# A hybrid decoder layer: the overflow tile is computed ahead of the last expert, whose rows are added by TensorE

## The chip, the cores and the metric

The kernel runs on one core of a Trainium2 chip. The metric is the device time of one execution in microseconds (us), lower is better. Times are medians of a few runs; one more execution was recorded by the hardware profiler, and all rows below are of that one.

## The reference, cut to what matters

One decoder layer over 1024 positions of width 1024. After the token mixing (not touched here) comes a mixture of experts: each position picks 1 of 4 groups and in it 2 of 8 experts, 32 in all, with a hidden width of 128. All data are float32.

```
x  = x + gt1 * y                                   # token mixing
h2 = rms_norm(x, norm2_g) * (1 + sc2) + sh2
hg = einsum('nd,edf->nef', h2, w_gate)
hu = einsum('nd,edf->nef', h2, w_up)
act = silu(hg) * hu * gates                        # gates: 2 of 32 are not zero
x  = x + gt2 * einsum('nef,efd->nd', act, w_down)
return rms_norm(x, final_g)
```

## The kernel before

There is no scheduler: each engine has its own program, written out by hand, and the programs meet at semaphores. The order on an engine is the order of the code.

*Before the experts.* The rows x1 (the sum of input and token mixing) are stored in DRAM as `y_d`, their normed form as `xn2_d`. A router gives each expert a list of up to 128 positions (`tbl`, one column for each expert). What does not fit in an expert's 128 goes into overflow tiles: their lists are scattered to `far_d` during the expert loop and reloaded into further columns of `tbl`. Their number is `n_ov`, read from memory at run time. In the measured data the loop over them makes one turn.

*The expert loop*, 32 turns, `TURN[e]` being the expert of turn e. TensorE transposes the gathered 128 rows (`ex_t`), ScalarE and VectorE scale and shift them (`modulated`), TensorE makes the gate and up products (`ex_gu`: thirty-two 128x128 matmuls in the trace), ScalarE and VectorE the activation (`hidden`), TensorE the down product (`ex_dn`: two 128x512 products, four matmuls in the trace), VectorE multiplies by the router's gate and gt2 into `yo[e % 3]` (`result`), and GpSimd adds the rows to `y_d` by an indirect DMA (`scatter_add`). GpSimd also issues the gathers, up to four turns ahead (`gather_behind`). TensorE's order in a turn is transposes of e + 1, gate and up of e, down of e - 1.

*Weights.* SP issues three 512 KB transfers for each turn into a ring of 11 places (`load_expert`); a turn waits until all three have landed. For the overflow tile SP waits for `ov_go`, which GpSimd raises at turn 27, and loads into place 0.

*The overflow loop* follows turn 31 on every engine: gate and up, activation, down, scaling, scatter. The tile of E + 1, transposed in the loop for a next turn, holds no rows if there is none. Before its scatter GpSimd waits for all scatters of the 32 experts.

*The end.* When the overflow scatter has landed, `f_go` is raised, and SP reads `y_d` back in eight tiles of 128 rows into `x1[:, j]`. For each tile ScalarE squares and sums (1024 columns), for each pair of tiles VectorE adds EPS and GpSimd takes the power -0.5, VectorE scales each tile by the root and `final_g`, SP stores it.

`banks` is PSUM (8 banks, `PS[i]`); REG_P, REG_W, REG_Y and REG_S are large SBUF areas that many tiles share, so the trace names them and not the tiles. L792 is TensorE's `mm` helper, L1434 ScalarE's `fn`, L498 the direct weight loads, L500 those of the overflow tile, L531 the reload of `tbl`, L723 the gather, L729 the scatter, L2244 the scaling in `result`, L2281 the last scaling.

## Time and profile before

| | us |
|---|---|
| median of 3 runs (lowest to highest) | 873.35 (871.69 to 873.62) |
| profiled execution, its own time | 874.96 |
| its span, first to last instruction | 873.2 |
| TensorE busy in it | 815.8 |
| VectorE / ScalarE / GpSimd busy in it | 460.3 / 240.4 / 278.8 |

The span is what the trace shows; the execution's own time also has what lies around it. Positions in the trace are us from the span's start. The first 630 us are token mixing and router, the expert loop follows until about 834, then come the overflow tile and the end.

### The profile page before, as it was taken

Reading aid. Unit: us, or ns where it says so; the run is one execution under the profiler, and the core shown is the slowest. Engines: PE = TensorE matmul, PEld = TensorE weight load, DVE = VectorE, ACT = ScalarE, POOL = GpSimd, SP = SyncE. Lnnn points to the kernel's source line nnn. Section 1 sums busy time; section 2 is a strip of 40 time slices with the busy share of each in tenths; the row PEclk is TensorE's granted clock in tenths of the full one; section 3 lists DMA queues with packets and bytes.
Section 4 is the critical chain, followed back from the end, with each engine's and each line's share of the span. In section 5 each row is a group of like instructions: output and inputs, shape, how many; then the busy total and the mean of one; then the engine's idle time right before and its main releaser. Section 6 shows DMA issues by size and latency. Waiting matters only on the chain. (4 is left out here: it accounts for less than half of the span.)

```text
span 873.2 us, 17369 instructions
## 1 busy us (share of the span) xinstructions
PE 815.8 (93%) x7175; PEld 544.7 (62%) x7175; DVE 460.3 (53%) x1154; ACT 240.4 (28%) x581; POOL 278.8 (32%) x267
## 2 busy tenths in 40 slices
PE   8999999999999999799888999999999999999950
PEld 8557544544444355777777455555788888888830
DVE  3750478887830136467664244434645555454534
ACT  6220111112200143455543112221233223232214
POOL 5810000000499501452741100000135565543332
PEclk9999999999999999999999999999999999999995
DMA  9934433445111123000000881112889989888639
GB/s 315 324 90 135 145 120 121 139 158 172 37 38 36 27 70 133 18 3 4 4 4 20 308 325 48 49 73 96 325 296 301 303 285 273 277 267 261 206 73 367
DMA packets 79719, 136.35 MB, mean 156 GB/s; under 512 B 17213, under 2 KB 51226, under 8 KB 79642
## 3 DMA queue, kind: packets, MB, share of 16 engines
q1 hardware_dynamic: 69338, 118.44, 39.0%
q0 software_dynamic: 10304, 16.82, 8.2%
q8 instruction: 57, 0.93, 0.5%
q14 instruction: 20, 0.16, 0.1%
HBM read 124.18 MB, written 29.92 MB: 176 GB/s over the span
## 5 line engine op out<-in xcount | busy, mean ns | idle before, releaser
L792 PE MATMUL banks<-REG_W 128*128 128x512 f32 (+2 forms) x832 | 274.6, 499 | 0.9 <-DVE pend L1988 0.5
L792 PEld LDWEIGHTS banks<-REG_W 128*128 128x128 f32 (+1 forms) x832 | 125.9, 182 | 135.3 <-issue 133.8
L792 PE MATMUL banks<-REG_W,REG_Y 128*128 128x512 f32 x256 | 118.3, 599 | 1.4 <-DVE REG_Y L2236 1.1
L1434 ACT ACTIVATE REG_P<-banks 128x256 f32<-128x256 f32 (+2 forms) x126 | 53.5, 463 | 156.8 <-PE banks L792 137.7
L792 PE MATMUL banks<-REG_P 64*64 64x64 f32 (+3 forms) x2752 | 79.5, 230 | 13.1 <-issue 8.9
L792 PEld LDWEIGHTS banks<-REG_P 64*64 64x64 f32 (+1 forms) x2752 | 67.6, 135 | 23.0 <-issue 16.4
L1434 ACT ACTIVATE REG_Y<-banks,mod,s 128x128 f32<-128x128 f32 x136 | 51.2, 457 | 85.8 <-PE banks L1386 85.8
L792 PEld LDWEIGHTS banks<-REG_W,REG_Y 128*128 128x128 f32 x256 | 45.6, 191 | 44.3 <-issue 44.2
L792 PEld LDWEIGHTS banks<-REG_Y,REG_P 128*128 128x128 f32 (+1 forms) x616 | 63.1, 181 | 7.0 <-issue 7.0
L792 PE MATMUL banks<-REG_Y,REG_P 128*128 128x128 f32 (+1 forms) x616 | 66.6, 276 | 0.1
L636 POOL TENSOR_TENSOR REG_P<-REG_P 128x1040 f32<-128x1040 f32 x2 | 4.8, 2390 | 175.8 <-DVE REG_P L1801 175.8
L792 PE MATMUL banks<-REG_Y,REG_W 128*128 128x128 f32 x512 | 59.9, 275 | 0.2 <-DVE REG_Y L2105 0.2
L792 PEld LDWEIGHTS banks<-REG_Y,REG_W 128*128 128x128 f32 x512 | 58.4, 192 | 1.1 <-DMA REG_W<-in_moe_w_down 1.1
L1715 DVE SCALAR_TENSOR_TENSOR REG_Y<-REG_P,cc,REG_Y 128x256 f32<-128x256 f32 x112 | 54.3, 485 | 4.0
L729 POOL DMA_INDIRECT y_d<-REG_Y,tbl x22 | 34.9, 1589 | 60.0 <-DVE REG_Y L2244 60.0
L678 POOL TENSOR_TENSOR REG_P<-REG_P,lmask 128x512 f32<-128x512 f32 x20 | 26.3, 1322 | 79.7 <-DVE REG_P L2014 79.7
L792 PE MATMUL banks<-REG_P,REG_Y 128*128 128x512 f32 x112 | 51.4, 592 | 0.0
L2105 DVE TENSOR_SCALAR REG_Y<-banks,s,mod 128x128 f32<-128x128 f32 x136 | 46.2, 403 | 2.0 <-PE banks L1386 2.0
L579 POOL TENSOR_SCALAR ss<-ss 128x1 f32<-128x1 f32 x16 | 3.6, 224 | 135.9 <-ACT REG_P L1434 127.8
L2233 DVE SCALAR_TENSOR_TENSOR REG_Y<-REG_Y,banks 128x128 f32<-128x128 f32 x33 | 9.5, 288 | 70.8 <-ACT REG_Y L1434 70.8
L2244 DVE SCALAR_TENSOR_TENSOR REG_Y<-banks,tbl,gtb 128x512 f32<-128x512 f32 x46 | 32.4, 746 | 19.2 <-PE banks L792 19.2
L1434 ACT ACTIVATE REG_Y<-banks 128x128 f32<-128x128 f32 (+2 forms) x43 | 14.8, 345 | 88.4 <-PE banks L792 76.5
(295 smaller groups left out, 1108.1 us busy)
## 6 DMA issues: line engine op xcount, KB each, us to landing
REG_P<-in_w_ada SPq DMA_DIRECT2D x20, 1024.0 KB, 6.2
REG_W<-in_w_in SPq DMA_DIRECT2D x17, 512.0 KB
REG_P<-in_moe_w_gate SPq DMA_DIRECT2D x17, 512.0 KB, 8.3
REG_W<-in_moe_w_gate SPq DMA_DIRECT2D x16, 512.0 KB, 6.4
REG_W<-in_moe_w_up SPq DMA_DIRECT2D x16, 512.0 KB, 10.7
REG_W<-in_moe_w_down SPq DMA_DIRECT2D x16, 512.0 KB, 16.7
REG_P<-in_moe_w_up SPq DMA_DIRECT2D x14, 512.0 KB, 14.9
REG_P<-in_moe_w_down SPq DMA_DIRECT2D x12, 512.0 KB, 21.2
```

The lines of the kernel that those rows point to most:

```text
L579: ch.step(gp.tensor_scalar(sj, sj, EPS, None, ALU.add))
L636: ch.step(gp.tensor_tensor(zc, zc, yc, ALU.mult))
L678: gp.tensor_tensor(bl[:, l % 2], ab[:, :, 0, :], lmask[:, l:l + 1, :].to_broadcast([P, 8, CH]), ALU.mult)\
L729: gp.indirect_dma_start(out=y_d[:, :], out_offset=bass.IndirectOffsetOnAxis(ap=at, axis=0), in_=yo[b], in_offset=None, bounds_check=last_r ...
L792: return pe.matmul(o_, l, r, start=start, stop=stop, skip_group_check=True)
L1434: return act.activation(o_, i_, f, **kw)
L1715: last = stt(dst, src[:, k], cc[:, k:k + 1], dst, ALU.mult, ALU.add)
L2105: last = ts(dst[:, k, :], PS[bank][:, (k - 4) * P:(k - 3) * P], s2[:, k:k + 1], mod[:, M_SH2 + k:M_SH2 + k + 1], ALU.mult, ALU.add)
L2233: ch.step(stt(a1[:, par, :], th[:, par, :], 1.0, PS[2 + par][:, 0:P], ALU.add, ALU.mult))
L2244: last = stt(yo[b][:, h * 512:(h + 1) * 512], PS[4 + 2 * par + h][:, :], gate(TURN[e] if isinstance(e, int) else e), gtb[:, 1, h * 512:(h ...
```

## The change

What it does, engine by engine:

- The overflow loop stands between turn 30 and turn 31 (`LAST`). Its scaled rows go to `yo[2]`. The counts of its semaphores are one lower, those of turn 31 come after it.
- Turn 31 is not scattered. VectorE builds eight 128x128 matrices `hot[:, j]` of ones and zeros (1 where a row of expert 31's tile belongs to position p of tile j). After turn 31, TensorE multiplies `hot[:, j]` with expert 31's scaled rows into a pair of PSUM banks, for each of the eight tiles.
- For tiles 0, 2, 4, 5, 6, 7 VectorE adds that pair to the tile read back from `y_d` (`completed`). For tiles 1 and 3 (`ON_PE`) TensorE adds the tile itself, by a product with the identity (`reloaded`), and ScalarE and VectorE read the sum from PSUM.
- `y_d` is read back once the overflow scatter has landed (`ov_go`; `f_go` is gone).
- The roots are taken tile by tile on GpSimd, in two instructions each (`rstd`), where one served two tiles.
- The gather of the overflow tile is issued at turn 25 (before: 28), the reload of `tbl` ahead of the weights of turn 30 (before: ahead of those of turn 31), and the gather for the tile after it before the scatter of turn 30. `xg[3]` is cleared once.

```diff
@@ sp @@
             for e in range(RING, E):
                 sp.wait_ge(s["m_dn"], e - RING + 1)
-                load_expert(e % RING, TURN[e], s_w[e % RING])
                 if e == E - 2:
                     sp.wait_ge(s["far_tab"], 16 * 2 * NT)
                     sp.dma_start(tbl[:, E:TILES, :], far_d.rearrange("(p t) c -> p t c", t=OVT)).then_inc(s["far_ld"], 16)
+                load_expert(e % RING, TURN[e], s_w[e % RING])
...
-            sp.wait_ge(s["f_go"], 1)
+            sp.wait_ge(s["ov_go"], n_ov + 1)
@@ gpsimd @@
+            ch.step(gp.memset(xg[3], 0.0))
+            gather(TURN[3], 3)
...
-            for e in range(E):
+            for e in range(LAST):
+                if e == LAST - 1:
+                    gp.wait_ge(s["m_tx"], E + 1)
+                    gather(E + 1, 0)
                 gp.wait_ge(s["m_yd"], e + 1)
                 scatter_add(rows_of(TURN[e], 0), e % RES)
                 gather_behind(e + 3)
-                if e == E - 1:
-                    gp.wait_ge(s["m_tx"], E + 1)
-                    gather(E + 1, 0)
-                if e + BUF == E:
+                if e + 3 + BUF == E:
                     gp.wait_ge(s["far_ld"], 32)
                     gp.wait_ge(s["m_tx"], E - BUF + 1)
                     gather(E, 0)
...
+            for j in range(NT):
+                rstd(j, 2)
@@ tensor @@
             ex_t(E, 0, 16 * (E // BUF + 1))
-            ex_dn(E - 1, (E - 1) % 2, (E - 1) % RING)
+            ex_dn(LAST - 1, 0, (LAST - 1) % RING)
...
             with pe.Fori(0, n_ov) as i:
                 ex_gu(i + E, 0, 0, "m_", s["ov_w"], i * 48 + 48, False)
-                pe.wait_ge(s["m_yd"], i + E)
-                ex_dn(i + E, 0, 0, "m_", False)
                 ex_t(i + (E + 1), 0, i * 16 + 16 * (E // BUF + 2))
+                pe.wait_ge(s["m_yd"], i + LAST)
+                ex_dn(i + LAST, 0, 0, "m_", False)
+
+            ex_gu(LAST, 1, LAST % RING, wsem=s_w[LAST % RING], wcount=w_loads(LAST % RING, LAST // RING + 1), wait_free=False)
+            ex_dn(n_ov + LAST, 1, LAST % RING, wait_free=False)
+            beside(8, 2)
+            def placed(j):
+                q = 2 * ((j + 1) % 4)
...
+                if j - 4 in ON_PE:
+                    pe.wait_ge(s["f_o"], j - 3)
+                elif j >= 4:
+                    pe.wait_ge(s["op_x1"], NT + 1 + [i for i in FIN if i not in ON_PE].index(j - 4))
+                for h in range(2):
+                    if j == 0:
+                        pe.wait_ge(s["m_yd"], n_ov + (E + h))
+                    last = mm(PS[q + h][:, :], hot[:, j, :], yo[LAST % RES][:, h * 512:(h + 1) * 512], True, j not in ON_PE)
+                return last
+
+            def reloaded(j):
+                q = 2 * ((j + 1) % 4)
+                pe.wait_ge(s_w[j], w_loads(j, len(range(j, E, RING))) + 16)
+                for h in range(2):
+                    last = mm(PS[q + h][:, :], ident[:, :], x1[:, j, h * 512:(h + 1) * 512], False, True)
+                return last
@@ vector @@
+            ch.step(dve.tensor_copy(gap[:, 0:1], tbl[:, TURN[LAST], 0:1]))
+            ch.step(stt(left[:, :], i32[:, 0:NT], -float(P), gap[:, 0:1].to_broadcast([P, NT]), ALU.mult, ALU.add))
+            for j in range(NT):
+                ts(hot[:, j, :].rearrange("p (a b) -> p a b", a=KD), i128[:, :].rearrange("p (b a) -> p a b", a=KD), left[:, j:j + 1], None, ALU.is_equal)
...
+            def completed(j):
+                dve.wait_ge(s_w[j], w_loads(j, len(range(j, E, RING))) + 16)
+                dve.wait_ge(s["op_ps"], NT + 1 + FIN.index(j))
+                tt(x1[:, j], x1[:, j], pair(j), ALU.add).then_inc(s["op_x1"], 1)
```

How the order of instructions changes is shown at three places. First TensorE's queue of before, from the down products of turn 29 to the end. `ident` is the transpose of a tile, `128x512 x2` a down product; the names are of the SBUF areas.

```order
L792 MATMUL banks<-REG_W,REG_Y 128x512 x2
L792 MATMUL banks<-REG_Y,REG_P 128x128 x16
L792 MATMUL banks<-REG_S,REG_Y 128x512 x2
L1386 MATMUL banks<-ident,REG_Y 128x128 x8
L792 MATMUL banks<-REG_P,REG_Y 128x512 x2
L1423 TENSOR_LOAD idy
...
L792 MATMUL banks<-REG_Y,REG_W 128x128 x16
...
L792 MATMUL banks<-REG_W,REG_Y 128x512 x2
...
L1386 MATMUL banks<-ident,REG_Y 128x128 x8
```

The same stretch of the changed kernel, up to the placement of tile 3:

```order
L795 MATMUL banks<-REG_W,REG_Y 128x512 x2
L1389 MATMUL banks<-ident,REG_Y 128x128 x8
L795 MATMUL banks<-REG_S,REG_Y 128x512 x2
L1425 TENSOR_LOAD idy
...
L795 MATMUL banks<-REG_Y,REG_W 128x128 x16
...
L1389 MATMUL banks<-ident,REG_Y 128x128 x8
...
L795 MATMUL banks<-REG_W,REG_Y 128x512 x2
...
L795 MATMUL banks<-REG_Y,REG_P 128x128 x16
...
L795 MATMUL banks<-REG_P,REG_Y 128x512 x2
...
L795 MATMUL banks<-REG_Y,REG_W 128x512 x5
L795 MATMUL banks<-REG_P,ident 128x512 x2
L795 MATMUL banks<-REG_Y,REG_W 128x512 x2
```

Turn 31's gate and up products (`REG_Y,REG_P`, x16) have moved from ahead of turn 30's down product to behind the overflow tile, and its down product with them; the transposes in the loop stand ahead of the overflow tile's down product, and the 128x512 products at the end are new.

Second, VectorE's queue of the changed kernel from the scaling of turn 31 (L2280) on; in the kernel before, eight L2281 scalings and four L2273 additions stand there.

```order
L2280 SCALAR_TENSOR_TENSOR REG_Y<-banks,tbl,gtb 128x512 x2
L2328 TENSOR_TENSOR REG_P<-REG_P,banks 128x1024 x2
L2332 SCALAR_TENSOR_TENSOR REG_P<-REG_P,rs,gtb 128x1024
L2332 SCALAR_TENSOR_TENSOR REG_P<-banks,rs,gtb 128x1024
L2328 TENSOR_TENSOR REG_P<-REG_P,banks 128x1024
L2332 SCALAR_TENSOR_TENSOR REG_P<-REG_P,rs,gtb 128x1024
L2328 TENSOR_TENSOR REG_P<-REG_P,banks 128x1024
L2332 SCALAR_TENSOR_TENSOR REG_P<-banks,rs,gtb 128x1024
L2328 TENSOR_TENSOR REG_P<-REG_P,banks 128x1024
L2332 SCALAR_TENSOR_TENSOR REG_P<-REG_P,rs,gtb 128x1024
L2328 TENSOR_TENSOR REG_P<-REG_P,banks 128x1024
L2332 SCALAR_TENSOR_TENSOR REG_P<-REG_P,rs,gtb 128x1024 x3
```

The six additions (L2328) alternate with the eight last scalings (L2332); from tile 4's on there are four additions and six scalings. Third, SP's queue in the changed kernel, between the weights of turns 29 and 30; before, the row `tbl<-far_d` stood behind the row with REG_S.

```order
L503 DMA REG_W<-in_moe_w_down 128x1024
L535 DMA tbl<-far_d 128x30
L503 DMA REG_P<-in_moe_w_gate 128x1024
L503 DMA REG_Y<-in_moe_w_up 128x1024
L503 DMA REG_S<-in_moe_w_down 128x1024
```

The reload of `tbl` has moved ahead of the three transfers of turn 30.

## Rows read from the trace of the kernel before

**Rows 1.** Page of the profile: span, busy time of each engine, granted clock in 40 slices.
```profile
span 873.2 us, 17369 instructions
...
PE 815.8 (93%) x7175; PEld 544.7 (62%) x7175; DVE 460.3 (53%) x1154; ACT 240.4 (28%) x581; POOL 278.8 (32%) x267
...
PEclk9999999999999999999999999999999999999995
```

**Rows 2.** Timeline, 800 to 846 us: start us, duration us, engine, line, operation, count.
```profile
805.78 1.88 PE L792 MATMUL banks<-REG_P,REG_Y 128*128 128x512 f32 x4
807.50 1.04 PE L1386 MATMUL banks<-ident,REG_Y 128*128 128x128 f32 x8
...
823.59 1.06 POOL L723 DMA_INDIRECT REG_Y<-xn_d,tbl  x1 [0.30 <-issue]
...
824.28 1.88 PE L792 MATMUL banks<-REG_W,REG_Y 128*128 128x512 f32 x4
...
831.76 1.09 PE L1386 MATMUL banks<-ident,REG_Y 128*128 128x128 f32 x8
832.69 1.88 PE L792 MATMUL banks<-REG_P,REG_Y 128*128 128x512 f32 x4
834.80 3.83 PE L792 MATMUL banks<-REG_Y,REG_W 128*128 128x128 f32 x32 [0.24 <-DVE REG_Y L2105]
839.74 1.96 PE L792 MATMUL banks<-REG_W,REG_Y 128*128 128x512 f32 x4 [1.10 <-DVE REG_Y L2236]
...
841.95 1.41 DVE L2244 SCALAR_TENSOR_TENSOR REG_Y<-banks,tbl,gtb 128x512 f32<-128x512 f32 x2 [2.36 <-PE banks L792]
...
842.13 1.09 PE L1386 MATMUL banks<-ident,REG_Y 128*128 128x128 f32 x8 [0.43 <-DMA REG_Y<-xn_d,tbl]
...
843.79 1.60 POOL L729 DMA_INDIRECT y_d<-REG_Y,idx  x1 [0.16 <-issue]
```

**Rows 3.** Timeline of SP's queue, 783 to 820 us.
```profile
783.06 3.10 SPq L498 DMA_DIRECT2D REG_W<-in_moe_w_down  x1
...
793.65 1.63 SPq L531 DMA_DIRECT2D tbl<-far_d  x1
...
817.11 0.38 SPq L500 DMA_DIRECT2D REG_W<-in_moe_w_down  x1
```

**Rows 4.** DMA issues of 783, 793 and 816 us: count, KB, us to landing.
```profile
REG_W<-in_moe_w_down SPq DMA_DIRECT2D x1, 512.0 KB, 30.3
...
tbl<-far_d SPq DMA_DIRECT2D x1, 15.0 KB, 26.2
...
REG_W<-in_moe_w_down SPq DMA_DIRECT2D x1, 512.0 KB, 17.2
```

**Rows 5.** Windows: busy us of each engine, PEclk, DMA share, GB/s.
```profile
825.00:830.00 5.00, 4.85 (x36) 3.91 (x35) 1.78 (x4) 0.00 (x0) 1.57 (x1) 1.00 0.37 109
...
28.00:30.00 2.00, 2.00 (x4) 0.90 (x3) 1.93 (x4) 0.87 (x1) 1.73 (x5) 0.52 1.36 244
30.00:32.00 2.00, 2.00 (x4) 0.73 (x4) 1.93 (x3) 0.00 (x0) 1.73 (x5) 0.63 0.97 339
...
847.00:848.00 1.00, 0.00 (x0) 0.00 (x0) 0.00 (x0) 0.00 (x0) 0.12 (x1) 0.64 0.35 58
...
861.00:867.00 6.00, 0.00 (x0) 0.00 (x0) 6.00 (x8) 2.69 (x6) 3.32 (x2) 0.50 1.00 405
```

**Rows 6.** Timeline of the tail.
```profile
852.44 1.06 ACT L1434 ACTIVATE REG_W<-REG_P 128x1024 f32<-128x1024 f32 x1 [7.67 <-DMA REG_P<-y_d]
...
864.00 4.87 DVE L2281 SCALAR_TENSOR_TENSOR REG_P<-REG_P,rs,gtb 128x1024 f32<-128x1024 f32 x4
```

**Rows 7.** Timeline of TensorE at the start.
```profile
27.57 8.80 PE L792 MATMUL banks<-REG_W 128*128 128x512 f32 x16 [0.32 <-DVE REG_W L1755]
```

**Rows 8.** Two source lines: durations in ns, minimum, median, maximum, first and last start.
```profile
L2114 DVE TENSOR_TENSOR REG_P<-banks,REG_P x16: 680/686/693, 494.5 to 615.0; 128x512 f32<-128x512 f32 x16
...
L786 POOL TENSOR_TENSOR rs<-ss,mhalf x4: 731/1662/1664, 855.2 to 864.2; 128x2 f32<-128x2 f32 x4
```

More of the change, by code:

```diff
@@ L263, in build @@
         fsq, _ = area(REG_W, 0, 2, D)
+        hot, _ = area(REG_W, SLOT, NT, P)
+        LAST = E - 1
+        ON_PE = (1, 3)
+        FIN = (0, 2, 1, 3, 4, 5, 6, 7)
+        assert LAST % RING == 9 and LAST % RES == 1
         ident = sb("ident", [P, P])
@@ L741, in _ @@
             gp.wait_ge(s["st_x1"], 16 * NT)
-            for e in range(2, BUF):
-                gather(TURN[e], e)
+            gather(TURN[2], 2)
+            ch.step(gp.memset(xg[3], 0.0))
+            gather(TURN[3], 3)
             def gather_behind(e):
@@ L778, in _ @@
                 fetch(at, 0)
-                gp.wait_ge(s_sc[0], i * 16 + 16 * (len(range(0, E, RES)) + 1))
+                gp.wait_ge(s_sc[2], i * 16 + 16 * (len(range(2, LAST, RES)) + 1))
                 gp.sem_inc(s["ov_go"], 1)
-            gp.sem_inc(s["f_go"], 1)
-            for i in range(NT // 2):
-                gp.wait_ge(s["f_ss"], i + 1)
-                at = slice(2 * i, 2 * i + 2)
-                gp.tensor_tensor(rs[:, 2, at], ss[:, 2, at], mhalf[:, 0:2], ALU.pow).then_inc(s["rstd_ready"], 1)
+            for j in range(NT):
+                rstd(j, 2)
         @block.tensor
@@ L1672, in _ @@
             modulated(xt[:, 0], 0, 1, "m_tx", "m_xa", 0)
-            for e in range(E):
-                if e + 1 < E:
-                    modulated(xt[:, (e + 1) % 2], 0, e + 2, "m_tx", "m_xa", 0)
+            for e in range(LAST):
+                modulated(xt[:, (e + 1) % 2], 0, e + 2, "m_tx", "m_xa", 0)
                 hidden(e, e % 2, free=e >= 2)
@@ L2262, in _ @@
                 ch.enter(i, 1)
-                hidden(i + E, 0, free=False)
-                dve.wait_ge(s_sc[0], i * 16 + 16 * len(range(0, E, RES)))
-                result(i + E, 0)
+                hidden(i + LAST, 0, free=False)
+                dve.wait_ge(s["m_dn"], i + E)
+                dve.wait_ge(s_sc[2], i * 16 + 16 * len(range(2, LAST, RES)))
+                scaled_halves(2, 0, gate(i + E))[1].then_inc(s["m_yd"], 1)
                 modulated(xt[:, 0], i + (E + 2), "m_tx", "m_xd", 1)
-            dve.wait_ge(s["xr_ld"], 16 * (NT + 1))
@@ L2270, in root_args @@
-            def root_args(i):
-                dve.wait_ge(s["ss_ready"], 2 * NT + 2 * i + 2)
-                at = slice(2 * i, 2 * i + 2)
-                ts(ss[:, 2, at], ss[:, 2, at], EPS, None, ALU.add).then_inc(s["f_ss"], 1)
-            root_args(0)
-            for i in range(NT // 2):
-                if i + 1 < NT // 2:
-                    root_args(i + 1)
-                dve.wait_ge(s["rstd_ready"], 2 * NT + i + 1)
-                for j in (2 * i, 2 * i + 1):
-                    stt(x1[:, j], x1[:, j], rs[:, 2, j:j + 1], fg, ALU.mult, ALU.mult).then_inc(s["f_o"], 1)
+            ch.leave(n_ov)
@@ new lines, in _, with pair @@
+            hidden(n_ov + LAST, 1, free=False)
+            dve.wait_ge(s["m_dn"], n_ov + E)
+            dve.wait_ge(s_sc[LAST % RES], 16 * (LAST // RES))
+            for half in scaled_halves(LAST % RES, 1, gate(TURN[LAST])):
+                half.then_inc(s["m_yd"], 1)
+            def pair(j):
+                q = 2 * ((j + 1) % 4)
+                return banks[:, q:q + 2, :].rearrange("p a d -> p (a d)")
+            def completed(j):
+                dve.wait_ge(s_w[j], w_loads(j, len(range(j, E, RING))) + 16)
+                dve.wait_ge(s["op_ps"], NT + 1 + FIN.index(j))
+                tt(x1[:, j], x1[:, j], pair(j), ALU.add).then_inc(s["op_x1"], 1)
@@ new lines, in finished_rows @@
+            def finished_rows(j):
+                dve.wait_ge(s["rstd_ready"], 2 * NT + j + 1)
+                stt(x1[:, j], pair(j) if j in ON_PE else x1[:, j], rs[:, 2, j:j + 1], fg, ALU.mult, ALU.mult).then_inc(s["f_o"], 1)
+            completed(0)
+            dve.wait_ge(s["xr_ld"], 16 * (NT + 1))
+            completed(2)
+            finished_rows(0)
+            finished_rows(1)
+            completed(4)
+            finished_rows(2)
+            completed(5)
+            finished_rows(3)
@@ L2285 @@
+            completed(6)
+            finished_rows(4)
+            completed(7)
+            for j in range(5, NT):
+                finished_rows(j)
 _INS = ["x", "c", "w_ada", "b_ada", "norm1_g", "norm2_g", "w_in", "w_out", "pool_w", "pool_scale", "attn_sinks", "conv_w",
```

53 lines of the change are left out of this document (34 added, 19 removed).

## The prediction

> **What bounds the kernel now.** I read the head of the page first: TensorE is busy 93% of the span, and the granted clock is 9 tenths or more in 39 of the forty slices [rows 1]. So up to about 840 us TensorE is the bound, and behind it there is a tail. Then the timeline. In the steady loop one expert costs TensorE 6.17 us (the down products at 805.78 and 824.28 are three experts apart), and two 128x512 products start 1.72 us before what follows them (805.78 to 807.50), so one f32 product of that shape costs 0.86 us at full clock [rows 2]. The order of the end, by the same view: down products of expert 29 at 824.28, then expert 31's gate and up, expert 30's down products, transposes of the overflow tile at 831.76, expert 31's down products at 832.69, the overflow tile's gate and up at 834.80, its down products at 839.74 (1.96 us), its scaling on VectorE at 841.95 (1.41 us), its scatter at 843.79 [rows 2]. TensorE's last matmul ends at 843.22 [rows 2]. From there the chain is scatter, read-back of y_d, norm, store: the first tile is squared at 852.44, VectorE scales the last one until 868.87 [rows 6], and the span ends at 873.2 [rows 1], 4.3 us later.
>
> The reader should then look at the DMA queue, because the overflow tile needs weights of its own. SP issues them after expert 27; the third (down) transfer goes out at 817.11 [rows 3] and lands 17.2 us later [rows 4], at **834.3**. That is no matter of bandwidth: between 825 and 830 us the engines were on average 37% busy [rows 5]. Some of the sixteen are still working through old packets while the rest are empty, and a semaphore is full only when the last is done. The same lag is seen earlier: the table reload issued at 793.65 took 26.2 us for 15 KB, the down weights issued at 783.06 took 30.3 us [rows 3, 4]. The Trainium skill (DMA: Bandwidth & Descriptors, "Latency and other measured facts") says that two of the sixteen engines are usually slower in traces and guesses at software-generated traffic as the cause; these landings agree, and nothing in the sum hangs on it.
>
> **The change, part by part.**
>
> 1. *Overflow tile ahead of expert 31.* Without expert 31's products, TensorE does the overflow transposes at 824.28 + 1.72 = 826.0, expert 30's down products 0.93 us later (831.76 to 832.69 [rows 2]), until 828.8, and could start the overflow gate and up 3.04 us after the transposes (831.76 to 834.80 [rows 2]), at 829.0. But it waits for the weights. Their issue is not moved (still at expert 27), the lagging engine has the same bytes ahead of them, and the gather that is moved from expert 28 to 25 only passes earlier through the same engine. I take 834.3 + 0.2 = **834.5**; bounds 829.0 (no lag) and 836 (issued about 1.5 us later, see 4). So 5.5 us of TensorE idle appear where expert 31 stood, and its work falls behind the landing.
>
> 2. *Clock.* In the tail of before, TensorE stopped at 843.22 [rows 2], and the granted clock in the slice 847 to 848 is 0.64 [rows 5]: it fell from 2.4 to 1.2 GHz at 847.3, 4.1 us after the stop. The new gap is 5.7 us (828.8 to 834.5), so I expect a fall in it. What that costs is also in the trace: at the start, the slices 28 to 30 and 30 to 32 show 0.52 and 0.63 [rows 5], about 3.4 us at 1.2 GHz, and the sixteen matmul records from 27.57 took 8.80 us [rows 7] where eight products at 0.86 are 6.9. So **+1.9**; bounds 0 and +3.8 (all of the 3.83 us gate and up group at half rate).
>
> 3. *Chain of the overflow tile.* Gate and up 3.83 (834.80 row), pause for ScalarE and VectorE 1.1 (838.63 to 839.74), down 1.96 [rows 2]: 834.5 + 1.9 + 6.9 = 843.3, against 841.70 before. The dummy tile's transposes (1.09) now stand ahead of the down products and fit in the 1.1 pause. Scaling, scatter and read-back follow as before: the first y_d tile lands 1.6 later than 852.44, at 854.0. So the reads gain nothing: they no longer wait for expert 31, but they wait for the overflow scatter.
>
> 4. *Overflow gather at expert 25, table reload ahead of expert 30's weights.* The reload now queues behind the down weights issued at 783.06, which land at 813.4 [rows 3, 4]. The gather stood at 823.59 [rows 2]; three experts earlier is 805.1, when GpSimd reaches the wait, so the gather and the scatters of experts 26 and 27 stand behind it up to 8 us. The gather is still done before 826 (in its old place it was in use 8.2 us after its issue, at 831.76), and the scatter buffers have three turns. 0 on the path; if a scatter is late, VectorE's result and the SP order for the overflow weights (about 1.5 us) slip: that is the 836 above. Expert 30's weights move behind 15 KB: 0 to +0.6.
>
> 5. *Hot matrices on VectorE and the memset.* Ten small operations lie in the new wait for weights: 0. If that cover is gone (weights at 829), about 2 us of them would stand ahead of the overflow activations, but those only start 3.8 us later. The memset of 1024 columns stands on GpSimd's queue ahead of expert 3's gather, where the gathers run one to four experts ahead of TensorE; I have no row of that shape and take it as no longer than a scatter's issue (1.60 [rows 2]): 0, at most +1.6.
>
> 6. *Expert 31 afterwards.* Loop end 0.4 (841.70 to 842.13, where the next matmul began), gate and up 3.74 as in a steady turn, pause 1.1, down 1.88: 843.3 + 7.1 = 850.4; first half of the result 0.25 + 0.70 later (841.95 row: 1.41 for two): products can start at **851.4**. The eight warming matmuls end before that.
>
> 7. *Placement on TensorE.* Eight pairs 0.86 each and two more pairs for the tiles added wholly there. Tile 4 is the seventh pair in the order: 14 x 0.86 = 12.0, done at **863.4**. Tiles 0, 1 and 2 are through VectorE before that (0 lands at 854.0), so it stands idle until tile 4. This is the step I trust most: products and adds alternate, and only four bank pairs exist.
>
> 8. *VectorE to the end.* After tile 4's product come four additions (4, 5, 6, 7) and six scalings (2 to 7). A scaling costs 1.20 (4.87 for four, started back to back [rows 6]). A 1024-column addition from PSUM is not in the trace; bounds 1.20 (the scaling) and 1.37 (two of 0.686 [rows 8]), I take 1.25, nearer the scaling, since one start is saved. 5.0 + 7.2 = 12.2: 875.6.
>
> 9. *Roots tile by tile.* GpSimd now does two instructions per tile. In before a root took 0.73 alone and 1.66 beside VectorE's scaling [rows 8], so it was held about 0.9. Only tile 7's root is short of cover; I add **0.9**: 876.5. The lock rule of the Trainium skill (SBUF — State Buffer, "SBUF: two separate sides") says the same of a two-input VectorE operation: GpSimd is blocked until it ends. By the rule both instructions of tile 7 could be blocked, one full scaling each; by the row, one is. The sum goes by the row.
>
> 10. *Store.* 4.3 as before: **880.8**, against 873.2: **+7.6 us**. The profiled execution took 874.96 by its own time, 1.8 around its span; the median of the runs is 873.35. I add 7.6 to the median: **881.0**.
>
> **Rivals.**
>
> *The clock holds.* For it: 5.7 us is not much over 4.1, and the place of the fall may move. Then 881.0 - 1.9 = 879.1. Chance 0.20.
>
> *The weights are in time.* For it: gathers and scatters share the lagging engine, and their order changes from expert 25 on. Against: they landed 17.2 after issue with the engines mostly empty. TensorE then starts at 829.0: 881.0 - 1.9 - 5.5 = **873.6**, no change: what is gained in the reads (5.8 earlier) is paid in products and additions. Chance 0.13.
>
> *Faster: the tail goes at VectorE's pace.* As before, weights in time, and TensorE never late for VectorE. The first tile lands at 852.44 - 5.8 = 846.6; six additions and eight scalings 17.1, root 0.9, store 4.3: 868.9, or **869.1** by the median. It decides at tile 4's product: it would have to be done at 846.6 + 4.9 = 851.5, and step 7 without waits gives 863.4 - 7.4 = 856.0. For that a product would have to cost 0.54 instead of 0.86. For it: the DMA engines are at 1.00 in the tail of before [rows 5], so reads that start earlier do take load off it. Chance 0.06.
>
> *Both roots of tile 7 blocked, as the lock rule has it.* The scaling before it ends, then each instruction stands behind another: one more scaling, 881.0 + 1.2 = 882.2. For it: additions of two inputs now run in between. Against: after tile 6's scaling VectorE has nothing left to block with. Chance 0.08.
>
> **How the numbers follow.** Forecast (weights late, clock falls) 0.50, clock holds 0.20, both roots 0.08, weights in time 0.13, faster 0.06; 0.03 for something worse than 884. The predicted time is the likeliest, 881.0. Its own range is 879 to 883.5 (clock 0 to 3.8, addition +0.5, weights +1.5 not all at once). The range for 8 in 10 must reach to the case at 873.6: 873.5 to 884.0. About 0.2% (1.7 us) is what a measurement of this kernel can tell from no change: faster 0.07, the same 0.12, slower 0.81.
>
> **What would show it.** In the changed profile: a gap of TensorE of 5 to 6 us before the overflow gate and up matmuls, ended by a landing of the overflow down weights near 834; PEclk at half for about 3 us after it; y_d read at 850 to 852, no earlier than before; expert 31's products after the overflow tile; twenty 128x512 products at 0.86; VectorE without a gap from tile 4's addition on; last store issued near 876. Wrong if the overflow weights land by 830, if TensorE starts the placements before 846, or if VectorE is not the last in the chain.

## The result, and the profile after

The changed kernel takes 881.09 us (median of 4 runs, 879.72 to 881.39), the kernel before in the same series 872.52 us (4 runs, 871.14 to 873.62). The ratio is 1.0088, with a 95% interval from 1.0075 to 1.0101: slower by about 7.7 us (the two medians by themselves lie 8.6 apart). The forecast was 881.0.

The page of the changed kernel's profile (span, TensorE's busy time, granted clock in forty slices; before: [rows 1]):

```profile
span 879.6 us, 17520 instructions
...
PE 834.5 (95%) x7231; PEld 555.2 (63%) x7231; DVE 469.2 (53%) x1166; ACT 240.0 (27%) x581; POOL 280.7 (32%) x279
...
PEclk9999999999999999999999999999999999999897
```

TensorE is busy 18.7 us longer than before: 20.8 us more from the down products of expert 29 on (37.86 against 17.02), 2.1 less ahead of them. One slice near the end has 8 tenths of the clock. The place itself is in the timeline (start us, duration us, engine, line, what it does, count, and in brackets the idle time before it and who ended it):

```profile
821.47 1.88 PE L795 MATMUL banks<-REG_W,REG_Y 128*128 128x512 f32 x4
823.19 1.04 PE L1389 MATMUL banks<-ident,REG_Y 128*128 128x128 f32 x8
824.06 1.88 PE L795 MATMUL banks<-REG_S,REG_Y 128*128 128x512 f32 x4
...
827.69 2.02 DVE L2304 TENSOR_SCALAR REG_W<-i,left 128x128 f32<-128x128 f32 x8
...
831.96 5.75 PE L795 MATMUL banks<-REG_Y,REG_W 128*128 128x128 f32 x32 [6.01 <-DMA REG_W<-in_moe_w_down]
...
838.72 1.99 PE L795 MATMUL banks<-REG_W,REG_Y 128*128 128x512 f32 x4
840.54 3.73 PE L795 MATMUL banks<-REG_Y,REG_P 128*128 128x128 f32 x32
...
848.89 5.32 PE L795 MATMUL banks<-REG_Y,REG_W 128*128 128x512 f32 x12
...
851.28 1.22 DVE L2328 TENSOR_TENSOR REG_P<-REG_P,banks 128x1024 f32<-128x1024 f32 x1 [2.57 <-DMA REG_P<-y_d]
```

The reader is to see this order: down products of expert 29 (821.47), transposes of the overflow tile, down products of expert 30, then nothing for 6.01 us until the overflow tile's down weights land, then its gate and up products, which take 5.75 us where they took 3.83 [rows 2]. Expert 31 stands behind, at 840.54. The landing in the list of DMA issues (count, KB, us from issue to landing), and the windows around the gap (us, busy time of PE, PEld, DVE, ACT, POOL, granted clock, DMA share, GB/s):

```profile
REG_W<-in_moe_w_down SPq DMA_DIRECT2D x1, 512.0 KB, 17.6
```

```profile
826.00:828.00 2.00, 0.00 (x0) 0.00 (x0) 1.93 (x7) 0.00 (x0) 1.70 (x2) 1.00 0.67 127
828.00:830.00 2.00, 0.00 (x0) 0.00 (x0) 1.71 (x8) 0.00 (x0) 1.66 (x2) 0.79 0.60 117
830.00:832.00 2.00, 0.04 (x1) 0.04 (x1) 0.00 (x0) 0.00 (x0) 0.00 (x0) 0.50 0.78 117
832.00:834.00 2.00, 2.00 (x9) 2.00 (x10) 0.00 (x0) 0.00 (x0) 0.00 (x0) 0.50 0.49 92
834.00:836.00 2.00, 2.00 (x12) 2.00 (x11) 0.00 (x0) 0.00 (x0) 0.06 (x1) 0.50 0.06 10
836.00:838.00 2.00, 2.00 (x20) 2.00 (x20) 0.00 (x0) 0.25 (x1) 0.13 (x1) 1.00 0.00 0
```

The clock stood at 2.4 GHz when TensorE stopped at 825.9, was at 1.2 GHz from about 829.2 (0.79 in the window 828 to 830) until 836, and was back for the window 836 to 838. The same slow 17 us landing as in [rows 4] is there. The share of the DMA engines was 0.86, 1.05 and 0.95 in the three windows from 814 to 820, just behind the issue, and between 0.43 and 0.78 from there to the landing, so at first the engines were full and afterwards they were not. No view of these traces tells the sixteen apart; that some of them lag, as the prediction has it, is not shown.

The tail (timeline, first and last pieces):

```profile
861.18 1.22 DVE L2328 TENSOR_TENSOR REG_P<-REG_P,banks 128x1024 f32<-128x1024 f32 x1 [1.83 <-PE banks L795]
862.32 1.28 DVE L2332 SCALAR_TENSOR_TENSOR REG_P<-REG_P,rs,gtb 128x1024 f32<-128x1024 f32 x1
...
869.29 2.47 DVE L2332 SCALAR_TENSOR_TENSOR REG_P<-REG_P,rs,gtb 128x1024 f32<-128x1024 f32 x2
...
870.64 1.20 POOL L584 TENSOR_SCALAR ss<-ss 128x1 f32<-128x1 f32 x1 [1.45 <-ACT REG_W L1470]
871.93 0.57 POOL L585 TENSOR_TENSOR rs<-ss,mhalf 128x1 f32<-128x1 f32 x1
872.53 1.28 DVE L2332 SCALAR_TENSOR_TENSOR REG_P<-REG_P,rs,gtb 128x1024 f32<-128x1024 f32 x1 [0.77 <-POOL rs L585]
```

VectorE waits for tile 4's product until 861.18, then works without a gap to the last scaling but one, waits 0.77 for tile 7's root, and ends at 873.81. The span ends only 5.8 us later, where it was 4.3 before. Why, is in the instructions with which the program closes (one source line for all engines; duration ns, then first and last start us). First the kernel before, then the changed one:

```profile
L117 POOLq DRAIN  x1: 8659/8659/8659, 864.1 to 864.1; - x1
...
L117 SPq COMPARE_BRANCH  x1: 38/38/38, 872.8 to 872.8; - x1
```

```profile
L117 POOLq DRAIN  x1: 7486/7486/7486, 871.9 to 871.9; - x1
...
L117 SPq COMPARE_BRANCH  x1: 38/38/38, 876.5 to 876.5; - x1
...
L117 SPq EVENT_SEMAPHORE  x1: 17/17/17, 879.6 to 879.6; - x1
```

SP is through with the last store at 876.5 (its COMPARE_BRANCH stands behind that wait) and then stands 2.9 us. What comes in between is GpSimd's closing drain, from 871.9 to 879.4. Before, both came at 872.8: GpSimd's last root began at 864.2 and was held, so that it took 1.66 us [rows 8], and its drain ended 6.9 us after that. In the changed kernel it is 6.9 us too, from the end of tile 7's root at 872.50.

**A common clock for all traces.** The profiled executions run at different offsets by the time they reach the experts (the kernel before has the half-clock stretch at the start of [rows 5, 7], the changed one has not, and two other traces that have the tail of before, e10 and e4 below, reach them 2.6 and 2.1 us sooner than that of before). So I count from a mark that all have, the start of the down products of expert 29: 824.28 before, 821.47 changed. The span ends 48.9 us after the mark before and 58.1 after it changed: +9.2, while the medians say +8.6 and the ratio +7.7.

### The profile page after: what moved, and what is told of

Same layout as the page of the kernel before. It is cut to its first block, busy times and chain, and to the rows that moved or that the text cites. A ratio compares the mean times of both kernels' runs of the same rounds, so it can differ in the third digit from the quotient of the medians.

```text
span 879.6 us, 17520 instructions
## 1 busy us (share of the span) xinstructions
PE 834.5 (95%) x7231; PEld 555.2 (63%) x7231; DVE 469.2 (53%) x1166; ACT 240.0 (27%) x581; POOL 280.7 (32%) x279
## 4 chain that ended last, share of the span: by engine, by line
PE 40%; DVE 4%; issue 3%; DMA 3%; POOL 1%; ACT 0%; SPq 0%; POOLq 0%; DVEq 0%
PE banks L795 36%; PE banks L1389 3%; DMA REG_W<-in_moe_w_down 2%; PE banks L1320 1%; DMA y_d<-REG_P,idx 1%; POOL rs L585 0%; POOL ss L584 0%; ACT REG_P L1470 0%; DVE REG_Y L2280 0%; DVE REG_Y L2146 0%; DVE REG_P L2155 0%; DVE REG_P L2332 0%; POOL REG_P L683 0%; DVE REG_P L2046 0%; DVE REG_P L2252 0%
## 5 line engine op out<-in xcount | busy, mean ns | idle before, releaser
L795 PE MATMUL banks<-REG_Y,REG_W 128*128 128x128 f32 (+1 forms) x544 | 76.3, 299 | 7.5 <-DMA REG_W<-in_moe_w_down 6.0
L795 PEld LDWEIGHTS banks<-REG_Y,REG_W 128*128 128x128 f32 x544 | 66.3, 197 | 15.8 <-DMA REG_W<-in_moe_w_down 6.8
L584 POOL TENSOR_SCALAR ss<-ss 128x1 f32<-128x1 f32 x24 | 6.4, 265 | 153.9 <-ACT REG_P L1470 127.8
L2280 DVE SCALAR_TENSOR_TENSOR REG_Y<-banks,tbl,gtb 128x512 f32<-128x512 f32 x44 | 31.0, 746 | 18.1 <-PE banks L795 18.1
## 6 DMA issues: line engine op xcount, KB each, us to landing
REG_W<-in_moe_w_up SPq DMA_DIRECT2D x16, 512.0 KB, 10.5
REG_P<-in_moe_w_down SPq DMA_DIRECT2D x12, 512.0 KB, 20.8
```

The source lines that it names most:

```text
L584: ch.step(gp.tensor_scalar(sj, sj, EPS, None, ALU.add))
L795: return pe.matmul(o_, l, r, start=start, stop=stop, skip_group_check=True)
L2280: return [stt(yo[b][:, h * 512:(h + 1) * 512], PS[4 + 2 * par + h][:, :], by, gtb[:, 1, h * 512:(h + 1) * 512], ALU.mult, ALU.mult) for h ...
```

## The experiments

All runs in one table. Times in us after the mark, worked out from each trace: start and length of the overflow tile's gate and up products, start of the placement products, end of VectorE's last scaling, end of the span. The ratio is to the kernel before in the same series, with its 95% interval; the changed kernel was timed in the first series only, so a run is set against it by the two ratios.

| kernel | gate/up | length | placement | last scaling | span | ratio |
|---|---|---|---|---|---|---|
| before | 10.5 | 3.83 | | 44.6 | 48.9 | 1 |
| changed | 10.5 | 5.75 | 27.4 | 52.3 | 58.1 | 1.0088 (1.0075 to 1.0101) |
| e1_weights_first | 4.9 | 3.83 | 21.6 | 46.5 | 52.3 | 1.0078 (1.0064 to 1.0092) |
| e2_awake | 14.1 | 3.74 | 29.1 | 54.0 | 59.8 | 1.0131 (1.0114 to 1.0147) |
| e3_weights_sooner | 6.8 | 3.84 | 21.8 | 46.7 | 52.5 | 1.0070 (1.0049 to 1.0091) |
| e4_before_roots | 10.2 | 3.83 | | 46.6 | 52.5 | 1.0041 (1.0025 to 1.0057) |
| e5_late_on_pe | 8.7 | 5.46 | 25.4 | 46.7 | 52.2 | 1.0056 (1.0032 to 1.0080) |
| e7_awake_less | 10.1 | 3.84 | 25.1 | 50.2 | 56.0 | 1.0104 (1.0080 to 1.0129) |
| e8_last_roots_on_scalar | 12.7 | 5.61 | 29.5 | 53.8 | 56.9 | 1.0076 (1.0057 to 1.0095) |
| e9_all_together | 4.9 | 3.83 | 19.9 | 41.9 | 44.9 | 0.9970 (0.9956 to 0.9983) |
| e10_before_late_gpsimd | 10.1 | 3.83 | | 44.1 | 51.4 | 1.0038 (1.0020 to 1.0056) |
| e11_all_but_roots | 4.8 | 3.83 | 20.0 | 42.0 | 47.6 | 1.0010 (0.9996 to 1.0024) |
| e12_gather_at_28 | 12.3 | 4.17 | 27.7 | 52.6 | 58.4 | 1.0137 (1.0111 to 1.0163) |

### Are the weights late, and does it matter?

**e1_weights_first**, on the changed kernel. Expert 31's weights and `final_g` are loaded behind the overflow tile's, and GpSimd gives the sign for these four turns earlier:

```diff
-            for e in range(RING, E):
+            for e in range(RING, LAST):
...
+            sp.wait_ge(s["m_dn"], LAST - RING + 1)
+            load_expert(LAST % RING, TURN[LAST], s_w[LAST % RING])
...
-                if e == E - 5:
+                if e == E - 9:
                     gp.sem_inc(s["ov_go"], 1)
```

> The changed kernel, with the overflow tile's three weight transfers issued ahead of those of turn 31 (GpSimd raises its flag at turn 23 instead of 27). Late weights as the cause (the prediction's steps 1 and 2): they land in the place where turn 31's landed, about 6 us sooner, before TensorE is ready; no gap before the overflow gate and up, no clock fall, so 5.8 + 1.9 = 7.7 us less than the changed kernel: 873.4, within 2 us of the kernel before. Rival, the tail's products and additions are the whole cause and the gap is slack: within 1 us of the changed kernel, about 881.

Its timeline:

```profile
829.47 3.83 PE L797 MATMUL banks<-REG_Y,REG_W 128*128 128x128 f32 x32 [0.37 <-DVE REG_Y L2148]
830.10 1.06 POOL L730 DMA_INDIRECT REG_Y<-xn_d,tbl  x1 [0.31 <-issue]
...
835.19 1.09 PE L1391 MATMUL banks<-ident,REG_Y 128*128 128x128 f32 x8 [1.88 <-DMA REG_Y<-xn_d,tbl]
```

The wait is gone, the clock stays, and everything behind it comes 5.8 us sooner after the mark (7.7 were expected, and the new wait below takes 1.9 of them). A new wait shows: the dummy tile's transposes, which the change put ahead of the overflow down products, wait 1.88 us for a gather that GpSimd issued behind a scatter. In the timed runs little of the 5.8 is seen: the ratio is 1.0078, 0.9 us under the changed kernel and inside its interval. By its number that is what the rival expected, though the trace shows the rival's reason, slack in the gap, to be wrong. Part of the loss can be placed. The profiled execution reaches the mark at 824.62, where the changed kernel's is there at 821.47, so 3.15 of the 5.8 were lost ahead of it, where both run the same work: a stretch of token mixing that took 75.2 us in the changed kernel's trace (387.0 to 462.2) took 77.4 here, and the granted clock between 633 and 638 us was 0.66 here and 1.00 there. This execution, at 878.69, was the fastest of its six (others 880.5 to 882.4, at a mean granted clock of 0.991 or 0.992 where this one has 0.994). Where the others lose the rest, no trace shows.

**e3_weights_sooner** issues the same three transfers behind expert 31's weights but ahead of `final_g`, with the sign four turns earlier as in e1:

```diff
-            sp.wait_ge(s["m_dn"], E - 4)
-            sp.dma_start(fg, v["final_g"].rearrange("(o n) -> o n", o=1).to_broadcast([P, D])).then_inc(s["xr_ld"], 16)
             sp.wait_ge(s["rt_n"], 1)
...
                 load_expert(0, e, s["ov_w"])
+            sp.wait_ge(s["m_dn"], E - 4)
+            sp.dma_start(fg, v["final_g"].rearrange("(o n) -> o n", o=1).to_broadcast([P, D])).then_inc(s["xr_ld"], 16)
...
-                if e == E - 5:
+                if e == E - 9:
                     gp.sem_inc(s["ov_go"], 1)
```

> The changed kernel, with the overflow weights issued right behind those of turn 31 and ahead of final_g, about 10 us sooner than now. If a lagging DMA engine works through its packets in order (my theory), the weights land only by final_g's share sooner, 2.3 us: gap 3.7 instead of 6 us, 878.8, or 876.9 if the clock then holds. Rival, the issue is simply late and the time from issue to landing stays 17 us: they land 10 us sooner, no gap, 873.4.

```profile
831.62 3.84 PE L795 MATMUL banks<-REG_Y,REG_W 128*128 128x128 f32 x32 [2.29 <-DMA REG_W<-in_moe_w_down]
```

The gap shrinks to 2.3 us, the clock does not fall (3.84 us for gate and up), placement starts at 21.8. The same as e1 within 0.2 us, without the new wait, since the gather then has the gap to hide in. Neither account of the landing came out: the down weights were issued 7.4 us sooner after the mark and landed 3.7 sooner (21.3 us behind their issue, where the changed kernel has 17.6), which lies between the 2.3 and the 10 that were expected. The timed runs, at 1.0070, again show little of what the trace does; its execution too came late to the mark (824.85), with 78.1 us for the stretch that took the changed kernel 75.2.

### Does the clock fall in the gap, and what does it cost?

**e2_awake** and **e7_awake_less** keep TensorE at work in the gap, with 44 and (e7) 22 products of 128x128 that nobody reads. The edit of e2:

```diff
+            beside(44, 3)
             pe.wait_ge(s["rt_n"], 1)
             n_ov = pe.value_load(idy[0:1, 0:1], min_val=1, max_val=OVT)
```

> The changed kernel, with 44 dummy 128x128 products (about 4.8 us) in TensorE's gap before the overflow tile. The weights land as late as before, but the granted clock does not fall, so the gate and up matmuls take 3.8 instead of 5.75 us: 1.9 us less than the changed kernel, 879.2. Rival, the half clock is hidden because something else is late as well: no change, 881.1; the gate and up group would be shorter but the next step would wait.

> The changed kernel with 22 warming products (about 5.0 us) ahead of the overflow tile's gate and up products, half of what e2_awake had. Theory (the gap lets the clock fall): the products end about 831, before the weights land at 831.9, the gate and up group takes 3.8 instead of 5.75 us, and all behind it comes 1.9 us sooner: ratio 1.0067 where the changed kernel has 1.0088. Rival (the group is slow for another reason, such as late operands): it stays at 5.7 us and the ratio at 1.009.

One such f32 product is two records and takes 0.227 us, twice what I had reckoned, so in e2 the 44 took 9.99 us and delayed the group by some 4. It missed its question but has gate and up at 3.74. e7 asks it properly:

```profile
827.63 5.07 PE L795 MATMUL banks<-ident 128*128 128x128 f32 x44
833.40 3.84 PE L795 MATMUL banks<-REG_Y,REG_W 128*128 128x128 f32 x32 [0.70 <-DMA REG_W<-in_moe_w_down]
```

3.84 where the changed kernel has 5.75: the fall is the idle gap's doing, and it costs 1.9 us of that group. The placement starts 2.3 sooner after the mark, 0.4 of it because the weights landed sooner. The timed runs show no gain: 1.0104 where the theory had 1.0067 and the rival 1.009, and 1.0067 is outside the interval. They scatter widely: the three with a mean granted clock of 0.995 or 0.996, the profiled one among them, took 878.75 to 881.10, the other three, at 0.988 to 0.993, 881.75 to 886.07. So the 1.9 us are shown on traces and not in the median.

### The tiles that are completed on TensorE

**e5_late_on_pe** takes tiles 6 and 7 for that instead of 1 and 3, and goes through all tiles in order:

```diff
-        ON_PE = (1, 3)
-        FIN = (0, 2, 1, 3, 4, 5, 6, 7)
+        ON_PE = (6, 7)
+        FIN = tuple(range(8))
```

> The changed kernel with tiles 6 and 7 added wholly on TensorE instead of 1 and 3, all tiles in order. Steps 7 and 8 of the prediction (the chain is seven product pairs, then ten VectorE operations): tile 4's pair is done three pairs sooner, only one addition is left behind it, and the end is set by TensorE's ten pairs (17.2 us from 848.9), a square 1.2, a root 0.85 and a scaling 1.2: VectorE ends at 869.6 instead of 873.8, 4.2 us less: 876.9. Rival, the tail goes at the pace of the DMA engines (4 MB in, 4 MB out): no change, 881.

```profile
847.64 12.18 PE L795 MATMUL banks<-REG_Y,REG_W 128*128 128x512 f32 x28
859.66 1.88 PE L795 MATMUL banks<-REG_P,ident 128*128 128x512 f32 x4
```

Fourteen products, seven pairs, run back to back (28 records of the trace), no VectorE wait at tile 4 is left, and from the start of the placement to the last scaling it is 21.3 us instead of 24.9: -3.6, against 4.2 expected. The ratio goes from 1.0088 to 1.0056, about 2.8 us, with intervals that overlap a little. The trace has 5.9 less to the end of the span, but 2.0 of these are there before the placement starts, since the weights happened to land sooner (gate and up at 8.7, not 10.5). Its gap is the shortest that cost the clock:

```profile
831.00 5.46 PE L795 MATMUL banks<-REG_Y,REG_W 128*128 128x128 f32 x32 [4.26 <-DMA REG_W<-in_moe_w_down]
```

### The roots, and who closes the kernel

**e4_before_roots** is the kernel before with this part of the change alone (VectorE's additions of EPS go too, since GpSimd's first instruction of a root makes them):

```diff
-            for i in range(NT // 2):
-                gp.wait_ge(s["f_ss"], i + 1)
-                at = slice(2 * i, 2 * i + 2)
-                gp.tensor_tensor(rs[:, 2, at], ss[:, 2, at], mhalf[:, 0:2], ALU.pow).then_inc(s["rstd_ready"], 1)
+            for j in range(NT):
+                rstd(j, 2)
```

> The kernel before, with one edit: the roots of the tail are made tile by tile on GpSimd (two instructions each) instead of for two tiles at once. Theory A (the tail of the kernel before is bound by its transfers): from 850.3 to 871.6 us the sixteen engines move the 8.39 MB of the eight reads and eight stores at about 400 GB/s almost without a gap, so stores that are asked for sooner only wait in the queue: 0 to -0.4 us, ratio 0.9995 to 1.000. Theory B (VectorE's pace bounds it): the first scaling no longer waits for the second tile of a pair, about 2.7 us sooner, and so is the end: ratio 0.997.

Neither theory had this: slower, by 0.41%. The timeline shows one pattern to the end:

```profile
865.54 1.31 POOL L579 TENSOR_SCALAR ss<-ss 128x1 f32<-128x1 f32 x1
866.94 0.57 POOL L580 TENSOR_TENSOR rs<-ss,mhalf 128x1 f32<-128x1 f32 x1
...
867.54 1.28 DVE L2270 SCALAR_TENSOR_TENSOR REG_P<-REG_P,rs,gtb 128x1024 f32<-128x1024 f32 x1 [0.77 <-POOL rs L580]
```

GpSimd's first instruction is held until VectorE's scaling ends, the second runs alone, and VectorE waits 0.77 for it, at each tile: a scaling every 2.05 us, where four of them took 4.87 back to back [rows 6]. And GpSimd's last root now ends 45.3 us after the mark and not 41.5, so that its drain ends the span at 874.7, 2.8 us after SP was through with the last store.

**e10_before_late_gpsimd** adds to the kernel before one column of work that nobody reads:

```diff
+            gp.wait_ge(s["f_o"], NT)
+            gp.memset(junk[:, :], 0.0)
```

> The kernel before with one more GpSimd instruction at its very end: a memset of one column, once VectorE's last scaling is done. Nothing reads it. Theory C (every kernel closes 6.9 + 0.2 us after GpSimd's last instruction, or with the last store, whichever is later): the memset ends about 0.3 after the last scaling and the span 7.1 us after that, where it now ends 4.3 after the scaling: +3.1 us, ratio 1.0035. Theory D (only the last store's landing counts): one column is nothing, ratio 1.000.

Its trace, the instruction and the closing line:

```profile
865.84 0.10 POOL L788 MEMSET junk<- 128x1 f32 x1 [3.09 <-DVE REG_P L2283]
```

```profile
L117 POOLq DRAIN  x1: 7059/7059/7059, 865.8 to 865.8; - x1
L117 SPq COMPARE_BRANCH  x1: 38/38/38, 869.7 to 869.7; - x1
...
L117 SPq EVENT_SEMAPHORE  x1: 17/17/17, 873.0 to 873.0; - x1
```

A tenth of a microsecond of work, behind the last scaling, makes the kernel 0.38% slower (0.35% expected by theory C, nothing by D). The last store was done at 869.7; the span ends at 873.1, 7.2 after the memset.

**e8_last_roots_on_scalar** goes the other way on the changed kernel: for tiles 6 and 7 ScalarE takes the square root behind its square, VectorE the reciprocal ahead of the scaling.

```diff
-            for j in range(NT):
+            for j in range(6):
                 rstd(j, 2)
...
+                if j >= 6:
+                    act.wait_ge(s["ss_ready"], 2 * NT + j + 1)
+                    fn(rs[:, 2, j:j + 1], ss[:, 2, j:j + 1], ACT.Sqrt, bias=epsc[:, 0:1]).then_inc(s["f_rt"], 1)
...
+                dve.wait_ge(s["f_rt"], j - 5)
+                dve.reciprocal(rs[:, 2, j:j + 1], rs[:, 2, j:j + 1]).then_inc(s["f_rr"], 1)
```

> The changed kernel with the roots of tiles 6 and 7 taken from GpSimd: ScalarE takes the square root behind its own squares (its function loaded ahead of the tail), VectorE the reciprocal. Theory C (GpSimd closes the kernel: in every trace so far its closing drain ends 6.9 us after its last instruction and the span 0.2 us later, while the last store had landed 2.9 us before): the span ends 2.9 us after VectorE's last scaling instead of 5.8, and the last scaling starts about 0.4 sooner, so -3.3 us, ratio 1.0050. Theory D (the prediction's: the last store closes the kernel and only its landing was mis-sized): -0.4 us, ratio 1.0083, with the closing wait of 2.9 us still there.

```profile
875.05 1.28 DVE L2342 SCALAR_TENSOR_TENSOR REG_P<-REG_P,rs,gtb 128x1024 f32<-128x1024 f32 x1
```

```profile
L117 SPq COMPARE_BRANCH  x1: 38/38/38, 879.0 to 879.0; - x1
...
L117 SPq EVENT_SEMAPHORE  x1: 17/17/17, 879.4 to 879.4; - x1
```

The close behind the last scaling is 3.1 us instead of 5.8, and SP's 2.9 us are gone. The time fell by less, to 1.0076. Theory C had 1.0050, which is outside the interval, and theory D 1.0083, which is inside, so the timed runs don't speak for C here; the closing rows do. The trace says what took the rest in its execution: the overflow weights landed 2.2 us later after the mark than in the changed kernel, though nothing ahead of them is changed.

### The gather's place

**e12_gather_at_28** puts the overflow gather back to turn 28 of GpSimd's order in the changed kernel:

```diff
-                if e + 3 + BUF == E:
+                if e + BUF == E:
```

> The changed kernel with the overflow tile's gather back at turn 28 in GpSimd's order (step 4 of the prediction undone, the table reload stays early). The prediction has 0 for its place: GpSimd no longer waits 9 us for the table at turn 25, the gather may come about 2 us too late for the transposes at 823.2, and the wait for the weights hides that: ratio 1.009, as the changed kernel. Rival (the early gather and its wait make the scatters late, or the gather's place moves the landing of the weights): the wait ahead of gate and up is 2 us or more away from 6.0.

```profile
828.33 1.97 PE L1389 MATMUL banks<-ident,REG_Y 128*128 128x128 f32 x8 [5.26 <-DMA REG_Y<-xn_d,tbl]
830.09 3.62 PE L795 MATMUL banks<-REG_S,REG_Y 128*128 128x512 f32 x4
```

The gather took 8.1 us from its issue at 820.20, the transposes waited 5.26 for it, the clock fell there, and expert 30's down products ran at half rate. In this trace most of it hides in the wait for the weights (placement at 27.7 after the mark, not 27.4), yet the timed runs are 0.5% slower than the changed kernel's, where no change was expected (four runs; its trace shows 0.3 us of that, and where the rest goes is not shown). So the early gather is not a cost of the change; by the times it earns its place.

### Everything at once

**e9_all_together** has the edits of e1, e5 and e8 (with the roots of tiles 4 to 7 off GpSimd), and the dummy tile's gather one turn earlier:

```diff
-                if e == LAST - 1:
+                if e == LAST - 2:
                     gp.wait_ge(s["m_tx"], E + 1)
                     gather(E + 1, 0)
```

> The changed kernel with every suspected cost taken out at once: overflow weights ahead of the last expert's, the dummy tile's gather ahead of the scatter of turn 29 (in e1_weights_first TensorE waited 1.9 us for it), the tiles wholly on TensorE are 6 and 7 instead of 1 and 3, and the roots of tiles 4 to 7 on ScalarE and VectorE. From the rows: overflow gate and up at 829.5, its down products end at 836.4, the scatter has landed by 842.8, placement starts at 844.2, VectorE ends 21.3 us later (as in e5_late_on_pe) at 865.5, store and close 2.9: 868.4 on the scale on which the kernel before has 873.2, -4.8 us, ratio 0.9945. Theory D (no change from the roots): ratio 0.998. Rival (transfers bound the tail again: 8.39 MB take 21.3 us, from about 843.8): not before 866.8, ratio 0.993 at best.

**e11_all_but_roots** is the same with all roots on GpSimd.

> e9_all_together with all roots back on GpSimd as in the changed kernel. Theory C: VectorE's last scaling ends 0.7 us sooner than in e9 (41.2 us after the down products of expert 29 began, where e9 has 41.9: no reciprocals), but GpSimd's last root ends only 1.6 us before it, so the span ends 5.5 us behind VectorE instead of 3.1: +1.7 us on e9, ratio 0.999. Theory D: 0.7 us less than e9, ratio 0.996.

e9, the placement and the end:

```profile
843.15 12.18 PE L799 MATMUL banks<-REG_Y,REG_W 128*128 128x512 f32 x28
...
863.86 1.28 DVE L2341 SCALAR_TENSOR_TENSOR REG_P<-banks,rs,gtb 128x1024 f32<-128x1024 f32 x1
```

e11, the end of VectorE's work and of the program:

```profile
862.22 2.48 DVE L2331 SCALAR_TENSOR_TENSOR REG_P<-banks,rs,gtb 128x1024 f32<-128x1024 f32 x2 [0.77 <-POOL rs L587]
```

```profile
L117 POOLq DRAIN  x1: 7486/7486/7486, 862.5 to 862.5; - x1
...
L117 SPq EVENT_SEMAPHORE  x1: 17/17/17, 870.2 to 870.2; - x1
```

e9 beats both kernels: 870.27 us against 873.48 in its series, 0.3% less. Less was gained than I had worked out: 44.9 us from the mark to the end are 869.2 on the scale on which I had 868.4, and the ratio is 0.9970, not 0.9945; theory D's 0.998 is inside the interval. e11 ends its scalings at the same time after the mark (42.0 and 41.9) but closes 5.6 us later instead of 3.1, and is no faster than the kernel before; theory D's 0.996 is well outside its interval, C's 0.999 just outside. The two differ in the roots alone, and their intervals are apart.

e11 also settles in timed runs what e1 left open. Against e5 it has the weights ahead of expert 31's, and the dummy tile's gather a turn earlier; the ratio falls from 1.0056 to 1.0010, some 4 us, and the intervals don't meet.

## Why the prediction came out right, step by step

On the scale of the trace of before (2.81 us added to the changed kernel's times):

| step | predicted | measured |
|---|---|---|
| 1 overflow transposes | 826.0 | 826.0 |
| 1 gate and up start, after the landing | 834.5 | 834.8 |
| 2 clock, added to that group | +1.9 | +1.9 |
| 3 overflow down products end | 843.3 | 843.5 |
| 3 first tile of y_d in use | 854.0 | 854.1 |
| 6 placement starts | 851.4 | 851.7 |
| 7 VectorE goes on with tile 4 | 863.4 | 864.0 |
| 8, 9 last scaling ends | 876.5 | 876.6 |
| 10 span ends | 880.8 | 882.4 |

Steps 1 to 9 hold in the traces, each within 0.6 us. The weights were the reason for the gap (e1, e3), the idle gap the reason for the clock (e7), and the products of tile 4 the wait before the tail (e5). In step 2 the price came out by another split than the one I reckoned with: not some 3.4 us at 1.2 GHz but 6.8 (829.2 to 836.0), of which 4.0 fell on the group and the others on the gap, where they cost nothing. In step 4 GpSimd did wait, 9.13 us for the table, and nothing on the path noticed it; leaving the gather in its old place costs more (e12). In step 6 "the eight warming matmuls end before that" is wrong:

```profile
847.10 1.95 PE L795 MATMUL banks<-ident 128*128 128x128 f32 x16
847.30 1.41 DVE L2280 SCALAR_TENSOR_TENSOR REG_Y<-banks,tbl,gtb 128x512 f32<-128x512 f32 x2 [2.08 <-PE banks L795]
```

The placement starts at 848.89 with no wait, straight behind the warming matmuls, while the first half of expert 31's result was done near 848.0. By an estimate from these rows they hold the placement up by 0.6 to 0.8 us. Since the 0.4 us that I had put at the end of the overflow loop did not appear, the sum hides it. No run takes them out. In step 8 an addition takes 1.22 us, and a next instruction starts 1.13 later; a scaling gives way after 1.19. In step 9 one of the two instructions of tile 7 was held and VectorE waited 0.77 (0.9 predicted). "Both roots blocked" did not happen: the second ran in 0.57, since VectorE had nothing left to run.

Whether some of the sixteen DMA engines lag behind the others, as the prediction supposes and reads from the late landings, these traces can't tell, since no view keeps the engines apart, and e3's landing fits neither account. Only the landing itself, 17.6 us behind its issue, came as forecast.

**The term that was mis-sized is step 10.** "4.3 as before" was 5.8. I took the 4.3 us behind the last scaling for a store. They were the store's only by a tie with GpSimd's close, at 872.8 in both. In the changed kernel the store was even quicker: SP was through with it 2.7 us after the last scaling, 4.0 before. In the changed kernel the last scaling waits for GpSimd's last root, so the close comes at root + 6.9 + 0.2, whatever the store does. e10 shows it by adding to it, in trace and time. The closes of e8 and e9 (3.1 us) show it by taking it away, that of e11 (5.6) by putting it back.

That the median still fell on 881.0 is partly luck: I added +7.6 to a median of 873.35, while the medians of the series that was compared, 872.52 and 881.09, lie 8.6 apart. From the mark the trace pair has +9.2, which is the 1.5 of step 10 and small parts of the others more than forecast. The two whole spans differ by 6.4 only, because the profiled execution of before came to the mark 2.8 us later; a single pair of executions can be off by that much.

Of the rivals, the clock did not hold, and the weights were not in time. The order of the tiles through the banks, and not the weights, keeps VectorE from its own pace: with the weights in time but tiles 1 and 3 on TensorE (e1) the last scaling still ends 1.9 us later than before.

**What stays open.** The landing of the overflow weights, in kernels that ask for them in the same order, comes 8.7 to 12.7 us after the mark, and no trace tells what decides it. Executions of one kernel lie up to 7.3 us apart with no more than a mean clock to tell them by (e5, e7). Of the 5.8 us that e1's trace shows, its timed runs confirm none beyond their noise; that the weights' place is worth about 4 us in time rests on e11 against e5, and the clock's 1.9 us rests on traces alone. And why GpSimd's close takes 6.9 us was not looked into.

## What to carry to other kernels

Work put behind a transfer costs what the transfer still lacks, and here 1.9 us of lost clock besides: issue the weights of a step that is moved forward first, in the same edit. In a tail, look at which engine's closing instruction comes last and not only at the last store: here a memset of one column on GpSimd behind everything else cost 3.3 us. When a second engine completes part of the tiles, give it the last ones, so that the buffers that pass between both are free early.

## What the runs showed of the hardware that I had not expected

The drain with which GpSimd closes ended 6.9 to 7.0 us after its last instruction, the same whether that was a root (before, changed, e4, e11) or a memset of one column (e10); where it had ended early (e8, e9) the span ended 0.4 us behind SP's pass of the last store.

TensorE's granted clock held through gaps of 0.7 us (e7) and 2.3 us (e3). It fell in those of 5.3 (e12), 6.0 (changed) and 8.2 us (e8), and after that of 4.3 in e5: there it was still 1.00 until 831.25, a quarter of a microsecond after the group had begun at 831.00, and 0.50 from then to 834.66, so that gate and up took 5.46 us.

Two GpSimd instructions in place of one per root cost the kernel before its back-to-back scalings (e4): 2.05 us per tile instead of 1.2, because one of them is held behind VectorE's scaling and the other then holds VectorE up. The Trainium skill (SBUF — State Buffer, "SBUF: two separate sides") says that a GpSimd operation that reads SBUF is locked out while a VectorE operation with two SBUF inputs, as this scaling is, runs. These rows agree, with 1.31 us for an instruction that takes 0.22 to 0.25 alone.
